# Mixture-of-experts block: the last pair of experts written out behind the loop with halved fetches, and the first expert layer activated by column halves

## The reference, cut to what matters

```python
def clamped_swiglu(g, u):
    g = jnp.minimum(g, SWIGLU_LIMIT)
    u = jnp.clip(u, -SWIGLU_LIMIT, SWIGLU_LIMIT)
    return g * jax.nn.sigmoid(SWIGLU_ALPHA * g) * (u + 1)

def expert_block(args):
    xb, e = args                        # xb: the tokens of expert e
    hid = xb @ w1[e] + b1[e]            # w1[e]: 1024 x 2048, gate | up
    return clamped_swiglu(hid[:, :D_FF], hid[:, D_FF:]) @ w2[e] + b2[e]   # w2[e]: 1024 x 1024
```

## Time and profile before

| | us |
|---|---|
| median of 3 runs (1490.2 to 1490.95) | 1490.69 |
| the profiled execution's own time | 1488.16 |
| its span, first to last instruction | 1486.4 |
| PE busy | 1373.8 (92%) |
| DVE busy | 504.5 (34%) |
| ACT busy | 313.5 (21%) |
| DMA, mean over the span | 336 GB/s |

### The profile page before, as it was taken

How to read it: one execution, slowest core, us unless ns; L and a number is a source line. 1 busy time by engine, 2 the same in 40 slices (tenths; PEclk the granted TensorE clock), 3 DMA queues, 4 the chain that set the end, 5 groups by cost and what they waited for, 6 DMA issues and landing times.

```text
span 1486.4 us, 17524 instructions
## 1 busy us (share of the span) xinstructions
PE 1373.8 (92%) x6860; PEld 740.0 (50%) x6860; DVE 504.5 (34%) x900; ACT 313.5 (21%) x454; POOL 46.8 (3%) x74
## 2 busy tenths in 40 slices
PE   5998999999889899998899998998999899999998
PEld 2884455433324324334333343243333487889987
DVE  2846435113113112121131131121211347755566
ACT  3515233101101101001011010010110354544451
POOL 2000001100000000000000000000000201000000
PEclk9999999999999999999999999999999999999999
DMA  9319915999999999999999999999999873565540
GB/s 390 120 37 368 421 39 177 429 429 427 428 429 429 428 428 429 429 428 428 429 428 429 428 429 428 428 429 429 427 429 428 340 268 104 174 195 182 187 142 29
DMA packets 61898, 500.01 MB, mean 336 GB/s; under 512 B 5192, under 2 KB 21864, under 8 KB 34144
## 3 DMA queue, kind: packets, MB, share of 16 engines
q1 hardware_dynamic: 59616, 492.85, 80.6%
q0 software_dynamic: 2032, 6.05, 1.4%
q10 hardware_dynamic: 208, 0.54, 0.1%
HBM read 498.37 MB, written 1.05 MB: 336 GB/s over the span
## 4 chain that ended last, share of the span: by engine, by line
PE 65%; DMA 23%; DVE 7%; issue 3%; SPq 1%; ACT 1%; DVEq 0%; ACTq 0%; PEldq 0%
PE bank L1601 27%; DMA ring<-in_w 20%; PE bank L646 17%; PE bank L684 15%; DMA ring<-in_w_in 2%; PE bank L704 2%; DVE dk L759 1%; DVE mrows L763 1%; DVE dk L753 1%; PE bank L657 1%; PE bank L692 1%; PE bank L666 1%; SPq L546 1%; PE bank L1788 0%; SPq L599 0%
## 5 line engine op out<-in xcount | busy, mean ns | idle before, releaser
L646 PE MATMUL bank<-ring,xn 128*64 128x512 f32 x2048 | 467.9, 611 | 64.3 <-DMA ring<-in_w 64.2
L646 PEld LDWEIGHTS bank<-ring,xn 128*64 128x64 f32 x2048 | 161.9, 140 | 360.0 <-issue 359.9
L684 PE MATMUL bank<-ring,dq 128*64 128x512 f32 x1024 | 226.8, 595 | 0.0
L718 ACT ACTIVATE sq<-mrows 128x512 f32<-128x512 f32 x32 | 19.6, 630 | 772.2 <-DVE mrows L748 772.2
L748 DVE TENSOR_SCALAR mrows<-bank 128x512 f32<-128x512 f32 x32 | 20.6, 686 | 474.6 <-PE bank L646 474.6
L684 PEld LDWEIGHTS bank<-ring,dq 128*64 128x64 f32 x1024 | 70.6, 137 | 136.5 <-issue 136.5
L772 DVE TENSOR_TENSOR dk<-bank,bc 128x512 f32<-128x512 f32 x32 | 22.1, 692 | 236.2 <-PE bank L684 236.2
L501 DVE TENSOR_TENSOR w_lo<-ring,w_hi 128x2048 fp32r<-128x2048 f32 x34 | 77.6, 2291 | 33.1 <-ACT w_hi L496 33.1
L1601 PE MATMUL bank<-x_hi,w_hi 128*128 128x256 f32 x256 | 72.4, 283 | 0.8 <-DVE h_lo L1479 0.8
L1601 PE MATMUL bank<-x_hi,w_lo 128*128 128x256 f32 x256 | 72.4, 283 | 0.0
L1601 PE MATMUL bank<-h_lo,w_hi 128*128 128x256 f32 x256 | 72.4, 283 | 0.0
(11 more groups left out here) (433 smaller groups left out, 1512.2 us busy)
## 6 DMA issues: line engine op xcount, KB each, us to landing
ring<-in_w SPq DMA_DIRECT2D x192, 2048.0 KB, 17.1
ring<-in_w_ff SPq DMA_DIRECT2D x32, 1024.0 KB, 5.3
ring<-in_w_ada SPq DMA_DIRECT2D x24, 1024.0 KB, 16.6
ring<-in_w_out SPq DMA_DIRECT2D x8, 1024.0 KB, 10.5
ring<-in_w_in SPq DMA_DIRECT2D x8, 992.0 KB, 25.1
ring<-in_w_in SPq DMA_DIRECT2D x8, 640.0 KB, 11.3
ring<-in_w_ple_gate SPq DMA_DIRECT2D x4, 1024.0 KB, 4.8
xc<-in_ctx SPq DMA_DIRECT2D x1, 1024.0 KB, 4.8
```

The source lines that it names most:

```text
L646: m = pe.matmul(banks[bank_no][mine(i), :], gathered[:, k, mine(i)], rows_of(at + i, 2)[:, k % 2, q * 512:(q + 1) * 512], start=k == 0, st ...
L684: m = pe.matmul(banks[OUT_BANKS[c]][mine(i), :], actT[:, k, mine(i)], rows_of(8 + 2 * j + i, 4)[:, r, c * 512:(c + 1) * 512], start=k == 0 ...
L718: act.activation(sg[:, cols], gs[:, cols], ACT.Sigmoid, scale=ALPHA).then_inc(moe("sigmoid", which), 1)
```

## The change

It has three parts.
- In every pair, `hidden` takes the quarters in the order gate 0, up 0, gate 1, up 1 (`QUARTERS`) and signals `first_full` after the first two. DVE clips, forms and multiplies the first column half, then the second, instead of both gates, both ups, both products.
- The last pair is written out behind a loop of 15 on all engines, without the gather of a 17th pair: PE has no L630 there, ACT no copy of it, DVE no selection for it.
- In the last pair, sets 4 and 6 come as halves: four transfers of 1 MB in place of two of 2 MB, the first halves of both experts first. PE waits for the first halves (`half_landed_w1`, `half_landed_w2`), multiplies with them, then waits for the rest.

DVE, the activation, before: `mrows` and `dk` as above, waits in brackets.

The diff:

```diff
--- before.py
+++ after.py
@@ -585,9 +585,9 @@
             wait_read(eng, "rank")
             return eng.value_load(most_i[0:1, 0:1], min_val=0, max_val=T)
 
-        def pair_loads(sp, n, pair, which):
-
-            for i, (kind, k, second) in enumerate(PAIR_BLOCKS):
+        def pair_loads(sp, n, pair, which, halved=False):
+
+            for i, (kind, k, second) in enumerate(PAIR_BLOCKS[0:6] if halved else PAIR_BLOCKS):
                 expert = pair * 2 + second
                 if kind == "w1":
                     src = a["w1"][0, expert, k * 2 * P:(k + 1) * 2 * P, :].rearrange("(p r) n -> p (r n)", p=P)
@@ -599,6 +599,26 @@
                 sp.dma_start(ring[:, s:s + 2, :].rearrange("p a n -> p (a n)"), src)\
                     .then_inc(moe(f"block_landed{s // 2}", which), 16)
 
+        def last_loads(sp):
+
+            n = PAIRS - 1
+            pair_loads(sp, n, n, MAIN, halved=True)
+            for at, whole in ((6, False), (8, True), (10, False)):
+                for half in range(1 if whole else 2):
+                    for i in (at, at + 1):
+                        kind, k, second = PAIR_BLOCKS[i]
+                        r, name = (2, "w1") if kind == "w1" else (4, "w2")
+                        src = a[name][0, 2 * n + second, k * r * P:(k + 1) * r * P, :].rearrange("(p r) n -> p (r n)", p=P)
+                        s = block_slot(i)
+                        if half == 0:
+                            sp.wait_ge(sem("ring_freed"), n * PAIR_CHUNKS + N_FRONT + 2 * i + 2 - SLOTS)
+                        if whole:
+                            sp.dma_start(ring[:, s:s + 2, :].rearrange("p a n -> p (a n)"), src)\
+                                .then_inc(sem(f"block_landed{s // 2}"), 16)
+                        else:
+                            sp.dma_start(ring[:, s + half, :], src[:, half * SLOT:(half + 1) * SLOT])\
+                                .then_inc(sem(f"block_landed{s // 2}" if half else f"half_landed_{name}"), 16)
+
         def sp_overflow(sp):
             count_ = load_most(sp)
             with sp.If(count_ > CAP):
@@ -617,6 +637,8 @@
 
             s = block_slot(i)
             return ring[:, s:s + 2, :].rearrange("p a n -> p (a n)").rearrange("p (r n) -> p r n", r=rows)
+
+        QUARTERS = [(q, (GATE_BANKS + UP_BANKS)[q]) for q in (0, 2, 1, 3)]
 
         def gather(pe, n, which, y_read):
 
@@ -632,22 +654,24 @@
                 if k % 4 == 3:
                     m.then_inc(moe("xt_full", which), 1)
 
-        def hidden(pe, n, which):
+        def hidden(pe, n, which, halved=False):
 
             for k in range(KD):
                 at = k // 2 * 2
                 if k % 4 == 0:
                     pe.wait_ge(moe("xt_read", which), n * 2 + (k // 4 + 1))
-                if k % 2 == 0:
+                if halved and k == KD - 2:
+                    pe.wait_ge(sem("half_landed_w1"), 32)
+                elif k % 2 == 0 or halved and k == KD - 1:
                     for i in range(2):
                         block_landed(pe, n, at + i, which)
-                for q, bank_no in enumerate(GATE_BANKS + UP_BANKS):
+                for q, bank_no in QUARTERS:
                     for i in range(2):
                         m = pe.matmul(banks[bank_no][mine(i), :], gathered[:, k, mine(i)],
                                       rows_of(at + i, 2)[:, k % 2, q * 512:(q + 1) * 512],
                                       start=k == 0, stop=k == KD - 1, skip_group_check=True)
-                    if k == KD - 1 and q == 1:
-                        m.then_inc(moe("gate_full", which), 1)
+                    if k == KD - 1 and q == 2:
+                        m.then_inc(moe("first_full", which), 1)
                 if k % 2 == 1:
                     m.then_inc(moe("ring_freed", which), 4)
                 if k == 5:
@@ -658,7 +682,7 @@
                                       b1rows[:, q * 512:(q + 1) * 512].bitcast(F32R),
                                       start=False, stop=False, skip_group_check=True)
 
-        def pe_rest(pe, n, which, ahead):
+        def pe_rest(pe, n, which, ahead, halved=False):
             for half in range(2):
 
                 pe.wait_ge(moe("gated", which), n * 2 + (half + 1))
@@ -675,17 +699,22 @@
 
             for j in range(2):
                 pe.wait_ge(moe("act_read", which), n * 2 + (j + 1))
-                for i in range(2):
-                    block_landed(pe, n, 8 + 2 * j + i, which)
-                for c in range(2):
-                    for r in range(4):
+                parts = [(0, 1), (2, 3)] if halved and j == 1 else [(0, 1, 2, 3)]
+                for part in parts:
+                    if len(parts) == 2 and part[0] == 0:
+                        pe.wait_ge(sem("half_landed_w2"), 32)
+                    else:
                         for i in range(2):
-                            k = 4 * j + r
-                            m = pe.matmul(banks[OUT_BANKS[c]][mine(i), :], actT[:, k, mine(i)],
-                                          rows_of(8 + 2 * j + i, 4)[:, r, c * 512:(c + 1) * 512],
-                                          start=k == 0, stop=k == KD - 1, skip_group_check=True)
-                    if j == 1 and c == 0:
-                        m.then_inc(moe("out_half", which), 1)
+                            block_landed(pe, n, 8 + 2 * j + i, which)
+                    for c in range(2):
+                        for r in part:
+                            for i in range(2):
+                                k = 4 * j + r
+                                m = pe.matmul(banks[OUT_BANKS[c]][mine(i), :], actT[:, k, mine(i)],
+                                              rows_of(8 + 2 * j + i, 4)[:, r, c * 512:(c + 1) * 512],
+                                              start=k == 0, stop=k == KD - 1, skip_group_check=True)
+                        if j == 1 and c == 0 and part[-1] == 3:
+                            m.then_inc(moe("out_half", which), 1)
                 m.then_inc(moe("ring_freed", which), 4)
                 if j == 0:
                     for c in range(2):
@@ -743,17 +772,16 @@
             dve.tensor_scalar(pick[:].bitcast(F32R), ahead, evens[:, bass.ds(pair, 1)], None, ALU.is_equal)\
                 .then_inc(moe("selg_ready", which), 1)
 
-            dve.wait_ge(moe("gate_full", which), n + 1)
-            for half in range(2):
-                dve.tensor_scalar(gs[:, half * 512:half * 512 + 512], banks[GATE_BANKS[half]][:], LIMIT, None, ALU.min)\
-                    .then_inc(moe("gate_clipped", which), 1)
-            dve.wait_ge(moe("ring_freed", which), freed_by(n, 2 * KD - 1, which))
             for half in range(2):
                 cols = slice(half * 512, half * 512 + 512)
+                if half == 0:
+                    dve.wait_ge(moe("first_full", which), n + 1)
+                else:
+                    dve.wait_ge(moe("ring_freed", which), freed_by(n, 2 * KD - 1, which))
+                dve.tensor_scalar(gs[:, cols], banks[GATE_BANKS[half]][:], LIMIT, None, ALU.min)\
+                    .then_inc(moe("gate_clipped", which), 1)
                 dve.tensor_scalar(us[:, cols], banks[UP_BANKS[half]][:], LIMIT, -LIMIT, ALU.min, ALU.max)\
                     .then_inc(moe("up_clipped", which), 1)
-            for half in range(2):
-                cols = slice(half * 512, half * 512 + 512)
                 dve.wait_ge(moe("gate_clipped", which), n * 2 + (half + 1))
                 dve.wait_ge(moe("up_clipped", which), n * 2 + (half + 1))
                 dve.scalar_tensor_tensor(out=us[:, cols], in0=us[:, cols], scalar=1.0, in1=gs[:, cols],
@@ -787,8 +815,9 @@
             sp.dma_start(xc[:, 2:4, :], a["x"][0].rearrange("(t p) d -> p t d", p=P)).then_inc(sem("x_in"), 16)
             for chunk in FRONT:
                 load_chunk(sp, chunk)
-            with sp.Fori(0, PAIRS) as pair:
+            with sp.Fori(0, PAIRS - 1) as pair:
                 pair_loads(sp, pair, pair, MAIN)
+            last_loads(sp)
             sp_overflow(sp)
             for chunk in BACK:
                 load_chunk(sp, chunk)
@@ -1029,10 +1058,12 @@
             for rows, raw in ((b1rows, b1raw), (b2rows, b2raw)):
                 step(act.activation(rows[:].bitcast(F32R), raw, ACT.Copy), "bias_rounded", wait=False)
             most_act = load_most(act)
-            with act.Fori(0, PAIRS) as pair:
+            with act.Fori(0, PAIRS - 1) as pair:
                 sigmoids(act, pair, MAIN)
                 gather_out(act, pair + 1, MAIN)
                 act_rest(act, pair, MAIN)
+            sigmoids(act, PAIRS - 1, MAIN)
+            act_rest(act, PAIRS - 1, MAIN)
             with act.If(most_act > CAP):
                 with act.Fori(1, ROUNDS) as r:
                     with act.If(most_act > r * CAP):
@@ -1444,10 +1475,11 @@
                 step(V.tensor_tensor(rows[E:2 * E, :].bitcast(F32R), raw[E:2 * E, :], rows[E:2 * E, :], ALU.subtract),
                      "bias_split", wait=False)
```

(7 more changed lines are left out.)

## The result

Over 22 executions each, the changed kernel takes 1492.71 us (median; 1489.88 to 1495.99), the kernel before 1490.24 us. The ratio is 1.0015, with a 95% interval of 1.0009 to 1.0022: 1.3 to 3.3 us slower, a difference that is there; its median lies within the 0.2% (3.0 us) named in the prediction, and the interval reaches just beyond.

The account below looks back on a forecast made before the run. DMA loads bound the loop until set 3 of the last pair, then PE, with DVE between. Terms sum to +1.05 us (low clock in set 3) or -0.53 (high), weighted +0.42: 1491.1 us, range 1488.4 to 1493.2.

Parts of the forecast that it names:

- The loop hides everything up to set 3: First 15 pairs: PE, DVE or ACT savings are waited away at the next load; only from set 3 on counts.
- The activation, -0.25: DVE in the last pair: the new order removes a pause, so the activation ends 0.25 us earlier.
- The hole brings the clock down: Between `hidden` and second turning, last pair: without the gather PE idles 3.8 of 4.6 us, so its clock falls.
- The signs named for it: Changed profile: second turning about 4.6 us behind `hidden`, set 5 above 7.09 us, first L704 38.1 us behind slow set 3.
- What the clock costs, 1.3 us, between 0.9 and 1.7: Last pair after the hole: one 3.4 us low stretch, its beginning free inside the hole, costs 1.3 us.
- the bound of 3.0: Upper bound on the clock's cost, 3.0 us, if it takes almost two low stretches to come back.
- Halves of set 4, 0 in nine cases and -1.58 in six: Ahead of set 4, last pair: saves 0 with low clock in set 3, 1.58 us with high; weighted 9 and 6.
- Halves of set 6: Last pair's set 6: PE comes when all of it is there, so 0; they would cover if PE were early.
- size of transfers: Last pair's halved loads: smaller rows cost 0.4 us at the end of set 6, inside 3.5 us slack, so 0.
- leaving the loop early: Entering the written-out last pair costs 0; up to 3.68 us would be hidden by gaps ahead of sets 2 and 3.
- The wait behind the pair: Behind the last pair: the 3.58 us gap stays; its low stretch may differ by up to 0.8 us either way.
- The rival with a price per transfer: Last pair's four added transfers cost up to 2.4 us each, +5.4 us, 1496.1 us; chance 0.05.

Follow-up runs that it names:

- e3: Kernel before with only the new order of quarters and activation; loop of 16, whole blocks, gather in every pair. 1490.58 us against 1490.08, ratio 1.0005.
- e1: Changed kernel plus sixteen unused matmuls between the last pair's first layer and its turning. 1490.09 us against 1490.08 for the kernel before, ratio 1.0005.
- e2: Kernel before with only the last pair written out on PE, ACT and DVE without the 17th gather. 1492.18 us against 1490.08, ratio 1.0019.
- g3: Changed kernel with unused matmuls in the hole and ahead of set 3, PE's over-64-token jump moved into the hole. 1494.40 us against 1489.53, ratio 1.0029.
- e4: Changed kernel with whole blocks instead of halves in the last pair. 1493.08 us against 1490.08 for the kernel before, ratio 1.0018.
- f1: Changed kernel plus unused matmuls: twelve in the last pair's hole, eight ahead of its set 3. 1489.87 us against 1489.55 for the kernel before, ratio 0.9998.
- f3: As f1, plus ten small unused matmuls behind the last pair, ahead of the turning of the tokens. 1492.95 us against 1489.55, ratio 1.0017.
- g2: Changed kernel with sixteen unused matmuls in the hole, PE's over-64-token jump moved behind them. 1494.45 us against 1489.53 for the kernel before, ratio 1.0036.
- f2: As f1, but with whole blocks in the last pair. 1490.94 us against 1489.55 for the kernel before, ratio 1.0010.
- t1: Kernel before plus ten small unused matmuls behind the last pair. 1492.20 us against 1489.55, ratio 1.0019.
- g1: Kernel before without TensorE's branch and code behind the loop for experts with over 64 tokens. 1489.28 us against 1489.53, ratio 0.9998.

## Why the prediction was right, and which terms were off

The time moved 2.5 us in the medians, 1.3 to 3.3 by the ratio, where +0.42 was forecast. It is inside the range, but with some luck: 2.5 us on the 1490.69 that I started from would be 1493.2, the upper end. The kernel before came out 0.45 us lower over 22 executions. The mechanism was right, and two terms were off to the same side: the low clock cost 1.7 us more than I took, and the 0.6 us that I counted on average for the halves of set 4 did not come. Step by step:

*The loop hides everything up to set 3.* Right: e3 and the 9.79 us between sets.

*The activation, -0.25.* Right: -0.21 in the changed kernel, -0.14 and -0.11 in e1 and e3.

*The hole brings the clock down.* Right, and shown by e1 and e2 from both sides. The signs named for it came too, the turning 4.67 us behind the end of `hidden` and set 5 above 7.09 us; but the mix came 39.85 us behind the start of set 3, not 38.1.

*What the clock costs, 1.3 us, between 0.9 and 1.7.* This term failed. It measured 2.96 us in the changed kernel (2.51 on set 5, 0.45 on the turning) and 2.84 in e2. I had reasoned that one low stretch lasts 3.4 us, as after set 3, and that part of it would fall into the hole. It lasted 6.8 us, as only the bound of 3.0 allowed. The traces show when this happened. All seven low stretches of 6.8 us in them have PE standing idle after the clock fell, before it worked again: 0.71 us in the changed kernel, 0.84 in e2, 1.6 in g3 at the same place; 0.81 in e4, 0.95 in f1, 1.6 in f3 and 0.74 in g3 behind the pair. In set 3 PE was at work when the clock fell, and at this hole it stood for 0.47 us after it in e4 and 0.35 in g2: 3.4 us each time. So I had that part wrong: a beginning inside the hole did not make the stretch cheaper in the changed kernel, it went with the long one. Why is not shown, and no run varied it alone.

*Halves of set 4, 0 in nine cases and -1.58 in six.* The sizes were right (f1 against f2: 1.64 us), the weights wrong. In all nine traces without filling ahead of it (before, changed, e1 to e4, t1, g1, g2), set 3 of the last pair took 8.78 us or 8.79. Drawn at 9 in 15 that would come about once in a hundred times, and the pairs are no draws. In the kernel before, from the second pair on, their third sets run slow, two high, three slow, two high, three slow, two high, two slow. The trace that I had read already showed it. The same run of three and two is in nearly all of every trace, shifted by a pair or two, and in the nine the last pair fell into its slow part. It need not: in g3 the twelfth to fourteenth pair are slow and the fifteenth is high, so by the same order the last would most likely have been high without the filling. What sets the order stays open. With set 3 slow the sum is -0.21 + 2.96 = +2.75 us, and +2.76 was measured to the mix.

*Halves of set 6, size of transfers, leaving the loop early:* all 0, as forecast; no run took them one by one. In f1, where PE was early, the halves of set 6 did cover: PE came at 1170.54, by 9.79 us a set the whole would have been there at 1171.7, and it did not wait. PE leaves the loop for the last pair without a gap (L733 at 1120.90 for 3.89 us, the next L670 at 1124.73). The evidence I gave for it was poor, though: DVE crossing its branch in 0.64 us says nothing of PE, whose code in that branch is long, and PE's crossing cost 3.4 us in the same place.

*The wait behind the pair* was read as one for DVE. It was PE's branch (t1, g1). The sum did not use it, so nothing hung on it.

*The rival with a price per transfer* is refuted at the size that would matter. e4 has four transfers fewer and is no faster. In f1 PE wanted the last halves at 1174.05, 2.3 us behind the 1171.7 of above, and did not wait; so four more transfers cost less than 0.6 us each, by estimate. The Trainium skill, "DMA: Bandwidth & Descriptors", section "Anatomy of one DMA", gives its 2.0 us for a single DMA on the path through GpSimd; these loads are issued by SP and stand in a full queue. Paid one after the other it does not hold for them: the sets stay 9.79 us apart.

## What to carry to other kernels

Useless work on TensorE can be holding its clock up. Before it is removed, look at what is idle on both sides of it and whether a stretch at the low clock would then fall on work that the end waits for; here 3.84 us of matmuls for a result that nobody reads were worth 2.9 us in the traces. And outcomes seen across iterations must not be used as odds for one of them before they are laid out in order: here they came in a regular pattern, and the last iteration sat in its slow part in nine traces of nine.

## What the runs showed of the hardware that I had not expected

- After a hole of 4.7 us with 0.9 us of turning in it, TensorE's clock stayed low for 6.8 us in the changed kernel and in e2, and for 3.4 us in e4. That cost 3.0, 2.8 and 1.4 us. From 300 us to the start of the second block the fourteen traces have 147 low stretches: 140 last 3.4 us and seven 6.8.
- A branch of TensorE that jumps over the long code of a case not taken was followed by 3.4 to 3.8 us between two of its matmuls in every kernel that has it behind the pair, and 4.1 to 4.2 us where it stood right behind issued matmuls (g2, g3). Matmuls issued ahead did not cover it. Its next signal came 3.7 us behind the mix with the branch and 0.4 without (g1). The profile put that wait down to VectorE. What takes the time in the jump, and whether the length of the code matters, was not tried.
- The gap of 1.58 us ahead of set 4 was followed by the low clock in the third pair of the changed kernel and in the eighth of t1 (8.65 us each); in the kernel before never.
